# mLSTM readout: the epsilon and the negated mean of each tile's normalisation move from VectorE to GpSimd

## The chip, the cores and the metric

The kernel runs on one core of a Trainium2 chip. The metric is device time in microseconds (us) of one launch. Before the change the median of three runs is 2130.13 us (2129.56, 2130.13 and 2136.0). Engines are called as in the profile: PE (TensorE, with PEld for its weight loads), DVE (VectorE), ACT (ScalarE), POOL (GpSimd) and SP (SyncE, which issues the DMAs).

## What is computed

The kernel is one transformer block in float32: a gated feed-forward layer, a token mixer and a second feed-forward layer, over 1024 latent rows of 1024 values and 256 context rows. The mixer joins a bidirectional mLSTM with 4 heads of 128 and a banded attention with 8 heads, and multiplies the joined rows by an output matrix. The change touches only the readout of the mLSTM: each row of each head is normalised over its 128 values, and multiplied by a gain and an output gate.

```python
def _mlstm_readout(h, o_pre, g):
    mu = h.mean(-1, keepdims=True)
    var = jnp.square(h - mu).mean(-1, keepdims=True)
    hn = ((h - mu) * lax.rsqrt(var + LN_EPS)).reshape(B, T, M_WIDTH)
    return (hn * g * jax.nn.sigmoid(o_pre.astype(F32))).astype(o_pre.dtype)
...
y_l = jnp.concatenate([m_l, a_l], -1) @ w_out
```

## The kernel before

Every engine has one hand-written program, and the engines meet through semaphores. Rows are handled in tiles of 128, eight of them latent; `y_m` holds the mLSTM's output, 8 tiles of 4 heads by 128.

The mLSTM runs 16 latent steps (`for i in range(LAST)`), forward and backward in turn, so that tiles are finished in pairs from step 8 on. In a step, POOL scales the queries (`scaled`, L2836) and multiplies the scores by the decays (`probabilities`, L2844). PE multiplies queries by the state, updates the state and multiplies scores by values (all in the helper at L3078). ACT decays the state (L2907). DVE adds the update to the state (`carry`, L2997) and divides the sums by their denominators into `y_m` (`divide`, L3008 to L3018). PE starts step `i` only when the division of step `i - 2` has been done (`h_read`, as the steps share two PSUM regions) and when the carried state of two updates before is there.

The readout of a tile `q` (0 to 7, in the order `TILES_READ`) goes over three engines. Its parts are set into the engines' orders by hand:

- DVE, `stats_dve(q)`: four `bn_stats` (L2975) and four `bn_aggr` (L2982), one for each head, which leave mean and variance side by side in a small buffer; then a wait for the last of these, and two `scalar_tensor_tensor` of 128x4: minus the mean into `offset` (L2985) and the variance plus epsilon into `rate` (L2986). The last one raises `read_measured`. Tiles 0, 1 and 2 come in steps 10, 12 and 14, after `divide` and ahead of `carry`; tile 3 after the loop; 4 to 7 in `output_dve`, between the `out_row_low` instructions (L3249) that make the low parts of the rows for the output product. Two slots of the small buffer alternate, and from tile 2 on the aggregation waits for the normalisation of tile `q - 2`.
- POOL, `invert_pool(q)`: `rate` to the power of minus a half (L2870), a wait for that, and `offset` times `rate` (L2873); it raises `read_inverted` once for each.
- ACT, `readout_act(q)`: waits for both, and scales and shifts each head's rows in place (L2922, four instructions); it raises `read_normed`.
- POOL, `gated_pool(q)`: `y_m` times the gate rows `o_in` (L2879, 128x512); it raises `read_done`, which releases the load of the gate rows two tiles on (SP, `o_row_sp`) and PE's transposes.

POOL's order is: `scaled` and `probabilities` of steps 0 to 13, `invert_pool(0)`, those of step 14, `gated_pool(0)`, `invert_pool(1)`, those of step 15, `gated_pool(1)`, and then `invert_pool` and `gated_pool` of each tile from 2 to 7. ACT's order has `readout_act(0)` between the state's decays of steps 12 and 13, and `readout_act(1)` after that of step 13; from tile 4 on the readouts stand among the `row_high` instructions (L3207) and the two copies of the gate row (L3212).

On PE the output product (L3326 to L3328) follows the steps. Its first three parts use the attention's rows. Then come the transposes of `y_m` (`turn_rows`, L3312): those of units 4 and 5 wait for the gating of tile 3, and those of units 12 to 15, in the middle of the fifth output tile, for the gating of tile 7. After the output product come a normalisation and the second feed-forward layer.

Of the kernel before, what the change touches and what calls it, by code (L numbers as in the profile page):

```python
# [7 lines left out]
P = 128  # L8
# [3 lines left out]
ALU = mybir.AluOpType  # L12
# [13 lines left out]
LN_EPS = 1e-5  # L26
# [5 lines left out]
M_HEADS, M_DH, M_WIDTH = 4, 128, 512  # L32
# [18 lines left out]
def hybrid_block(nc, x, c, ctx, c_ctx, w_ada, b_ada, ln_g, ln_b, ffn_w13, ffn_w2, w_in, b_gates,  # L51
                 conv_w, conv_b, mh_norm_g, attn_sink, w_out, rope_cs, out):
    with ExitStack() as keep:
# [3 lines left out]
        def sem(name):  # L57
            return keep.enter_context(nc.semaphore(name))
# [25 lines left out]
        ones, minus_half = consts[:, 0:1], consts[:, 1:2]  # L84
# [2433 lines left out]
        def core_step(dve, instruction):  # L2518
            cstep[0] += 1
            instruction.then_inc(cores_step, 1)  # L2520
            dve.wait_ge(cores_step, cstep[0])
# [201 lines left out]
        read_measured = sem("read_measured")  # L2723
        read_inverted = sem("read_inverted")
# [104 lines left out]
        def mlstm_pool(pool):  # L2829
# [33 lines left out]
            for q in range(2, TL):  # L2863
                invert_pool(pool, q)
                gated_pool(pool, q)

        def invert_pool(pool, q):
            _, rate, offset = read_slots(q)
            pool.wait_ge(read_measured, q + 1)
            nc.gpsimd.tensor_tensor(rate, rate, minus_half[:, 0:1].to_broadcast([P, M_HEADS]), ALU.pow)\  # L2870
                .then_inc(read_inverted, 1)
            pool.wait_ge(read_inverted, 2 * q + 1)
            nc.gpsimd.tensor_tensor(offset, offset, rate, ALU.mult).then_inc(read_inverted, 1)  # L2873

        def gated_pool(pool, q):
# [34 lines left out]
        def read_slots(i):  # L2910

            at = 32 + 16 * (i % 2)
            return small[:, at:at + 8], small[:, at + 8:at + 12], small[:, at + 12:at + 16]

        def readout_act(act, q):

            t = TILES_READ[q]
            _, rate, offset = read_slots(q)
            act.wait_ge(read_inverted, 2 * q + 2)
            for h in range(M_HEADS):  # L2920
                rows = y_m[:, t, h * M_DH:(h + 1) * M_DH]
                last = nc.scalar.activation(rows, rows, ACT.Identity, bias=offset[:, h:h + 1], scale=rate[:, h:h + 1])  # L2922
            last.then_inc(read_normed, 1)
# [43 lines left out]
        def stats_dve(dve, q):  # L2967

            t = TILES_READ[q]
            dve.wait_ge(h_read, 1 + max(i for i in range(LAST) if STEPS[LAT0 + i][1] == t))  # L2970
            st = small[:, 8:32]
            mv, rate, offset = read_slots(q)
            by_head = mv.rearrange("p (h c) -> p h c", c=2)
            for h in range(M_HEADS):
                nc.vector.bn_stats(st[:, 6 * h:6 * h + 6], y_m[:, t, h * M_DH:(h + 1) * M_DH])\  # L2975
                    .then_inc(cores_step, 1)
                cstep[0] += 1
            dve.wait_ge(cores_step, cstep[0])
            if q >= 2:
                dve.wait_ge(read_normed, q - 1)  # L2980
            for h in range(M_HEADS):
                last = nc.vector.bn_aggr(mv[:, 2 * h:2 * h + 2], st[:, 6 * h:6 * h + 6])  # L2982
            core_step(dve, last)
            unit = ones.to_broadcast([P, M_HEADS])
            nc.vector.scalar_tensor_tensor(offset, by_head[:, :, 0], -1.0, unit, op0=ALU.mult, op1=ALU.mult)  # L2985
            nc.vector.scalar_tensor_tensor(rate, by_head[:, :, 1], LN_EPS, unit, op0=ALU.add, op1=ALU.mult)\  # L2986
                .then_inc(read_measured, 1)

        def cores_dve(dve):
            def carry(n):  # L2990
# [260 lines left out]

        def output_dve(dve):
            stats_dve(dve, 4)
            stats_dve(dve, 5)
            out_row_low(dve, 4)
# [552 lines left out]
```

## Time and profile before

| what | value |
| --- | --- |
| median of 3 runs | 2130.13 us |
| the profiled execution: span from its first to its last instruction | 2127.8 us |
| median less this span (what lies around the span) | 2.3 us |
| PE busy | 2091.4 us (98%) |
| DVE busy | 1527.0 us (72%) |
| ACT busy | 905.6 us (43%) |
| POOL busy | 192.8 us (9%) |
| mean granted clock of PE | 0.996 of full speed |
| steps 10 to 15 and the readout | about 1357 to 1406 us of the span |

Times in the profile count from the start of the span. A row of the timeline is one instruction, or several equal ones in a row (xN), with its start, its length, its engine, line, operation and operands; in brackets stands how long the engine had been idle before it and what released it. The profiled execution is known by its span alone; its own time is taken as the span and the 2.3 us that lie around it, which is the median.

### The profile page before, as it was taken

How to read it: one execution, taken by the hardware profiler on the slowest of the kernel's cores; microseconds unless marked ns; L12 is line 12 of the kernel's file. 1: busy time of each engine (PE TensorE's matmuls, PEld its weight loads, DVE VectorE, ACT ScalarE, POOL GpSimd, SP SyncE). 2: the span in 40 equal slices, each digit the busy share in tenths (PEclk: the TensorE clock that was granted, in tenths of full speed). 3: DMA queues.
4: the chain of work that ended last, by engine and by line, in shares of the span. 5: the costliest groups of instructions: out<-in, count | busy, mean ns of one | idle time of the engine just before them, and what ended most of it. 6: DMA issues, size and time to landing. Idle time of an engine off the chain costs nothing.

```text
span 2127.8 us, 31643 instructions
## 1 busy us (share of the span) xinstructions
PE 2091.4 (98%) x11508; PEld 1768.0 (83%) x11510; DVE 1527.0 (72%) x2520; ACT 905.6 (43%) x1631; POOL 192.8 (9%) x212
## 2 busy tenths in 40 slices
PE   8999999999999999999999999999999999999998
PEld 4888888888888888899878878877888888888886
DVE  5778888777648878675665465866867777767787
ACT  4622222222237446542565555734532323336445
POOL 0000000000000001090111002821000000000001
PEclk9999999999999999999999999999999999999999
DMA  8144444555459664733231002732244434349773
GB/s 298 33 142 147 149 134 129 160 167 159 129 186 348 193 215 148 209 101 117 74 108 41 21 21 66 182 109 99 75 134 140 136 104 153 123 139 341 257 234 112
DMA packets 261841, 310.38 MB, mean 146 GB/s; under 512 B 19350, under 2 KB 164686, under 8 KB 261710
## 3 DMA queue, kind: packets, MB, share of 16 engines
q1 hardware_dynamic: 261422, 308.52, 45.4%
q8 instruction: 80, 1.31, 0.2%
q14 instruction: 51, 0.42, 0.1%
q10 hardware_dynamic: 288, 0.13, 0.0%
HBM read 242.13 MB, written 66.45 MB: 145 GB/s over the span
## 4 chain that ended last, share of the span: by engine, by line
PE 86%; DVE 4%; DMA 3%; ACT 2%; issue 1%; POOL 1%; SPq 1%; DVEq 0%; POOLq 0%; ACTq 0%
PE psum L1327 11%; PE psum L1328 11%; PE psum L1329 11%; PE psum L1527 6%; PE psum L1529 6%; PE psum L1528 6%; PE psum L2056 3%; PE psum L2058 3%; PE psum L2057 3%; PE psum L1347 2%; PE psum L1346 2%; PE psum L1345 2%; PE psum L3078 2%; PE psum L875 2%; PE psum L876 2%; PE psum L877 2%
## 5 line engine op out<-in xcount | busy, mean ns | idle before, releaser
L1327 PE MATMUL psum<-x_mix_h,x_op_h 128*128 128x512 f32 x640 | 251.2, 393 | 1.3 <-DVE v_sum L1135 1.2
L1328 PE MATMUL psum<-x_mix_l,x_op_h 128*128 128x512 f32 x640 | 249.8, 390 | 0.0
L1329 PE MATMUL psum<-x_mix_h,x_op_l 128*128 128x512 f32 x640 | 249.5, 390 | 0.0
L1527 PE MATMUL psum<-s_high 128*128 128x512 f32 x616 | 240.0, 390 | 0.3 <-DVE s_low L1514 0.3
L1528 PE MATMUL psum<-s_low,s_high 128*128 128x512 f32 x616 | 239.9, 389 | 0.0
L1529 PE MATMUL psum<-s_high,s_low 128*128 128x512 f32 x616 | 239.9, 389 | 0.0
L1514 DVE TENSOR_TENSOR s_low<-s_raw,s_high 128x1024 fp32r<-128x1024 f32 x154 | 186.9, 1217 | 50.5 <-ACT s_high L1475 50.5
L1475 ACT ACTIVATE s_high<-s_raw 128x1024 fp32r<-128x1024 f32 x154 | 161.3, 1057 | 124.1 <-PE psum L1529 56.3
L1019 ACT ACTIVATE x_op_h<-raw 128x512 fp32r<-128x512 f32 x140 | 86.1, 627 | 203.6 <-PE psum L1329 121.1
L1019 ACT ACTIVATE x_op_h<-w_sum 128x512 fp32r<-128x512 f32 x160 | 97.1, 625 | 162.9 <-DVE w_sum L997 107.1
L1327 PEld LDWEIGHTS psum<-x_mix_h,x_op_h 128*128 128x128 f32 x640 | 120.4, 188 | 25.4 <-issue 1.8
L1329 PEld LDWEIGHTS psum<-x_mix_h,x_op_l 128*128 128x128 f32 x640 | 120.2, 188 | 25.3
L1328 PEld LDWEIGHTS psum<-x_mix_l,x_op_h 128*128 128x128 f32 x640 | 120.4, 188 | 23.2
L1527 PEld LDWEIGHTS psum<-s_high 128*128 128x128 f32 x616 | 115.7, 188 | 24.5 <-DVE s_low L1514 0.8
L1529 PEld LDWEIGHTS psum<-s_high,s_low 128*128 128x128 f32 x616 | 115.7, 188 | 24.2
L1528 PEld LDWEIGHTS psum<-s_low,s_high 128*128 128x128 f32 x616 | 115.7, 188 | 23.9
L1025 DVE TENSOR_TENSOR x_op_l<-raw,x_op_h 128x512 fp32r<-128x512 f32 x140 | 92.8, 686 | 39.2 <-ACT x_op_h L1019 37.0
L2056 PE MATMUL psum<-p_wh,xh_lat 128*128 128x256 f32 x384 | 111.7, 291 | 0.0
L2057 PE MATMUL psum<-p_wl,xh_lat 128*128 128x256 f32 x384 | 108.8, 283 | 0.0
L2058 PE MATMUL psum<-p_wh,xl_lat 128*128 128x256 f32 x384 | 108.8, 283 | 0.0
L1025 DVE TENSOR_TENSOR x_op_l<-w_sum,x_op_h 128x512 fp32r<-128x512 f32 x160 | 107.5, 683 | 0.0
L773 DVE SCALAR_TENSOR_TENSOR ada_sums<-ada_slice,more,ada_sums 128x512 f32<-128x512 f32 x140 | 99.6, 746 | 3.7 <-DVE ada_sums L773 0.5
(408 smaller groups left out, 5069.6 us busy)
## 6 DMA issues: line engine op xcount, KB each, us to landing
raw<-in_ffn_w SPq DMA_DIRECT2D x88, 512.0 KB, 5.4
f_terms<-g_half SPq DMA_DIRECT2D x154, 256.0 KB, 2.3
s_raw<-f_terms SPq DMA_DIRECT2D x154, 256.0 KB, 3.2
s_raw<-in_ffn_w SPq DMA_DIRECT2D x154, 256.0 KB, 4.0
ada_slice<-in_w_ada SPq DMA_DIRECT2D x112, 256.0 KB, 3.1
c_raw<-in_ffn_w SPq DMA_DIRECT2D x22, 512.0 KB, 3.5
p_raw<-in_w_in SPq DMA_DIRECT2D x22, 512.0 KB, 4.0
early<-in_w_ada SPq DMA_DIRECT2D x16, 512.0 KB, 6.6
```

What stands on the lines that cost most here:

```text
L1019: nc.scalar.activation(op_tiles(F, op)[0][:], OP_SOURCE[op], ACT.Copy).then_inc(F.hi, 1)
L1025: nc.vector.tensor_tensor(low[:], OP_SOURCE[op], high[:].bitcast(F32), ALU.subtract).then_inc(F.lo, 1)
L1327: nc.tensor.matmul(o, wh[:, k], high(k), start=i < 4 and k == 0, stop=False, skip_group_check=i > 3)
L1328: nc.tensor.matmul(o, wh[:, k], low(k), start=False, stop=False, skip_group_check=i > 3)
L1329: last = nc.tensor.matmul(o, wl[:, k], high(k), start=False, stop=k == KH - 1, skip_group_check=i > 3)
L1514: nc.vector.tensor_tensor(S.low[s % RING][:], S.raw[s % RAWS][:], S.high[s % RING][:].bitcast(F32), ALU.subtract)\
L1527: nc.tensor.matmul(o, h[:, 0, rows], h[:, 1], start=i == 0 and q in (0, 1, 6), stop=False, skip_group_check=True)
L1528: nc.tensor.matmul(o, h[:, 0, rows], l[:, 1], start=False, stop=False, skip_group_check=True)
L1529: return nc.tensor.matmul(o, l[:, 0, rows], h[:, 1], start=False, stop=i == PAIRS - 1, skip_group_check=True)
L2056: nc.tensor.matmul(o[:, 0:w], high, high_w[:, k, :], start=k == 0, stop=False)
L2057: nc.tensor.matmul(o[:, 0:w], high, low_w[:, k, :], start=False, stop=False)
L2058: last = nc.tensor.matmul(o[:, 0:w], low, high_w[:, k, :], start=False, stop=k == KD - 1)
```

## The change

VectorE's part of a tile ends with the four aggregations; the last of them raises `read_measured`. The wait for them and the two small instructions L2985 and L2986 are gone. POOL does their work at the head of `invert_pool`: it adds epsilon to the variances (read with a step of two) into `rate`, and multiplies the means by -1 into `offset`; each raises `read_inverted`, so that this semaphore counts four for each tile in place of two. The power waits for the first of them, the product for both and the power. VectorE waits, ahead of a tile's `bn_stats`, until its own aggregations of the tile before have landed, since these read the buffer that `bn_stats` overwrites.

```diff
         def invert_pool(pool, q):
-            _, rate, offset = read_slots(q)
+            mv, rate, offset = read_slots(q)
+            by_head = mv.rearrange("p (h c) -> p h c", c=2)
             pool.wait_ge(read_measured, q + 1)
+            nc.gpsimd.tensor_scalar_add(rate, by_head[:, :, 1], LN_EPS).then_inc(read_inverted, 1)
+            nc.gpsimd.tensor_scalar_mul(offset, by_head[:, :, 0], -1.0).then_inc(read_inverted, 1)
+            pool.wait_ge(read_inverted, 4 * q + 1)
             nc.gpsimd.tensor_tensor(rate, rate, minus_half[:, 0:1].to_broadcast([P, M_HEADS]), ALU.pow)\
                 .then_inc(read_inverted, 1)
-            pool.wait_ge(read_inverted, 2 * q + 1)
+            pool.wait_ge(read_inverted, 4 * q + 3)
             nc.gpsimd.tensor_tensor(offset, offset, rate, ALU.mult).then_inc(read_inverted, 1)
...
-            act.wait_ge(read_inverted, 2 * q + 2)
+            act.wait_ge(read_inverted, 4 * q + 4)
...
-            mv, rate, offset = read_slots(q)
-            by_head = mv.rearrange("p (h c) -> p h c", c=2)
+            mv, _, _ = read_slots(q)
+            if q:
+                dve.wait_ge(read_measured, q)
             for h in range(M_HEADS):
                 nc.vector.bn_stats(st[:, 6 * h:6 * h + 6], y_m[:, t, h * M_DH:(h + 1) * M_DH])\
                     .then_inc(cores_step, 1)
...
-            core_step(dve, last)
-            unit = ones.to_broadcast([P, M_HEADS])
-            nc.vector.scalar_tensor_tensor(offset, by_head[:, :, 0], -1.0, unit, op0=ALU.mult, op1=ALU.mult)
-            nc.vector.scalar_tensor_tensor(rate, by_head[:, :, 1], LN_EPS, unit, op0=ALU.add, op1=ALU.mult)\
-                .then_inc(read_measured, 1)
+            last.then_inc(read_measured, 1)
```

## Rows read from the trace of the kernel before

**Rows 1.** The page, part 1: busy time, share of the span and instructions.

```profile
PE 2091.4 (98%) x11508; PEld 1768.0 (83%) x11510; DVE 1527.0 (72%) x2520; ACT 905.6 (43%) x1631; POOL 192.8 (9%) x212
```

**Rows 2.** Stretches: length, then busy time (instructions) by engine, clock, DMA.

```profile
1357.00:1406.00 49.00, 44.00 (x263) 38.63 (x261) 38.72 (x147) 29.43 (x74) 32.19 (x34) 0.97 0.28 88
...
1480.00:2127.80 647.80, 638.31 (x2839) 528.60 (x2837) 481.44 (x655) 258.69 (x387) 10.50 (x11) 1.00 0.49 161
```

**Rows 3.** PE's waits, 1340 to 1480 us: total us, times, longest.

```profile
PE psum L3078 <- issue: 4.7, 4, 3.8
PE psum L3312 <- POOL y_m L2879: 1.2, 2, 0.6
```

**Rows 4.** Timeline of DVE around the first tile's statistics.

```profile
1359.51 0.38 DVE L2982 BATCH_NORM_AGGREGATE small<-small 128x2 f32<-128x6 f32 x4
1359.92 3.55 DVE L2985 SCALAR_TENSOR_TENSOR small<-small,consts 128x4 f32<-128x4 f32 x1
...
1363.47 0.68 DVE L2997 TENSOR_TENSOR state<-psum,state 128x516 f32<-128x516 f32 x1
```

**Rows 5.** Instructions on the small buffer: ns min/median/max, first and last start.

```profile
L2985 DVE SCALAR_TENSOR_TENSOR small<-small,consts x8: 161/744/3546, 1359.9 to 1396.2; 128x4 f32<-128x4 f32 x8
L2986 DVE SCALAR_TENSOR_TENSOR small<-small,consts x8: 148/152/156, 1363.4 to 1397.0; 128x4 f32<-128x4 f32 x8
L2870 POOL TENSOR_TENSOR small<-small,consts x8: 1007/1023/1454, 1363.6 to 1401.5; 128x4 f32<-128x4 f32 x8
```

**Rows 6.** Timeline of POOL over the readout.

```profile
1359.72 1.28 POOL L2844 TENSOR_TENSOR d_rows<-scores,d_rows 128x512 f32<-128x512 f32 x1
...
1362.18 1.27 POOL L2844 TENSOR_TENSOR d_rows<-scores,d_rows 128x512 f32<-128x512 f32 x1
1363.62 1.03 POOL L2870 TENSOR_TENSOR small<-small,consts 128x4 f32<-128x4 f32 x1 [0.17 <-DVE small L2986]
...
1366.11 1.26 POOL L2844 TENSOR_TENSOR d_rows<-scores,d_rows 128x512 f32<-128x512 f32 x1
1369.96 1.27 POOL L2879 TENSOR_TENSOR y_m<-y_m,o_in 128x512 f32<-128x512 f32 x1 [2.59 <-ACT y_m L2922]
...
1376.64 1.39 POOL L2870 TENSOR_TENSOR small<-small,consts 128x4 f32<-128x4 f32 x1 [0.46 <-DVE small L2986]
...
1381.53 1.39 POOL L2870 TENSOR_TENSOR small<-small,consts 128x4 f32<-128x4 f32 x1 [0.17 <-DVE small L2986]
...
1384.97 1.28 POOL L2879 TENSOR_TENSOR y_m<-y_m,o_in 128x512 f32<-128x512 f32 x1 [1.77 <-ACT y_m L2922]
...
1391.50 1.29 POOL L2879 TENSOR_TENSOR y_m<-y_m,o_in 128x512 f32<-128x512 f32 x1 [3.79 <-ACT y_m L2922]
...
1404.97 1.29 POOL L2879 TENSOR_TENSOR y_m<-y_m,o_in 128x512 f32<-128x512 f32 x1 [1.77 <-ACT y_m L2922]
```

**Rows 7.** Timeline of ACT: the first and the fifth tile's normalisation.

```profile
1368.25 1.64 ACT L2922 ACTIVATE y_m<-y_m,small 128x128 f32<-128x128 f32 x4
...
1389.78 1.64 ACT L2922 ACTIVATE y_m<-y_m,small 128x128 f32<-128x128 f32 x4
```

**Rows 8.** Timeline of PE.

```profile
1365.89 1.13 PE L3078 MATMUL psum<-state,q_rows 128*128 128x129 f32 x8 [3.81 <-issue]
...
1377.31 0.47 PE L3326 MATMUL psum<-wo_h,xh_lat 128*128 128x512 f32 x1
...
1386.39 1.07 PE L3312 MATMUL psum<-ident,y_m 128*128 128x128 f32 x8 [0.64 <-POOL y_m L2879]
...
1406.40 1.50 PE L3312 MATMUL psum<-ident,y_m 128*128 128x128 f32 x12 [0.59 <-POOL y_m L2879]
```

**Rows 9.** Stretch after PE's stall: columns as in rows 2.

```profile
1366.00:1371.00 5.00, 5.00 (x31) 5.00 (x32) 4.62 (x23) 2.82 (x8) 2.41 (x3) 0.66 0.01 3
```

**Rows 10.** POOL's lines by form: count, busy us, mean ns, idle before.

```profile
L2873 POOL TENSOR_TENSOR small<-small 128x4 f32<-128x4 f32 x8 | 1.7, 216 | 0.6
...
L3599 POOL MEMSET consts<- 128x1 f32 x1 | 0.1, 98 | 0.0
```

## The prediction, made before the changed kernel was run

> **What bounds the kernel now.** I read the page first: PE is busy for 98% of the span and DVE for 72% [rows 1]. So work taken from DVE is worth something only where PE waits. The table by stretches shows where it can be. After 1480 us PE is busy for 638.31 of 647.80 us, and in the readout's stretch for 44.00 of 49.00 us [rows 2]; the 5.0 us left there, and a lower clock, are all that the change can win. PE's waits name what it waits for: 4.7 us in the mLSTM's steps, 3.8 us of it at once, and 1.2 us for GpSimd's gating [rows 3]. None of the rows of that view for 1340 to 1480 us names a transfer.
>
> The timelines then tell why. DVE ends the first tile's aggregation at 1359.89 us and starts L2985, an instruction of 128x4 that takes 3.55 us [rows 4], where the same takes 0.16 us at its shortest [rows 5]. It ends when POOL's row of 128x512 products ends, at 1362.18 + 1.27 = 1363.45 us [rows 6]. Behind it on DVE stand the state's addition (1363.47 us, rows 4), then a division, and PE starts its next step at 1365.89 us after 3.81 us of idleness [rows 8]. In the 5 us after that the granted clock is 0.66 on average [rows 9], between its two levels of 1.2 and 2.4 GHz: 5 x 0.34 = 1.7 us of work at full speed lost.
>
> So one instruction costs PE about 3.4 us and the clock 1.7 us. But a second chain runs beside it and decides what comes out: POOL inverts, ACT normalises, POOL gates, tile after tile, and PE waits for it twice, 0.64 us at 1386.39 us and 0.59 us at 1406.40 us [rows 8]. The change takes from the first and adds to the second.
>
> **What is removed.** Eight pairs on DVE of about 0.16 + 0.15 us [rows 5]. Seven pairs lie beside other work of DVE, ACT and POOL; the first holds the 3.4 us. What was behind it (addition, division, PE's step 12) starts about 3.45 us earlier, PE at 1362.4 us, and with an idle time of a few tenths the clock should stay up. The new wait ahead of `bn_stats` is for DVE's own aggregations of a tile before, mostly long done; only tiles 4 and 5 follow each other directly, and there it stands for the wait that was removed between aggregation and L2985 (0.03 us, rows 4). I cost it at nothing; what is queued behind it is only DVE's row work, which ACT or PE outlast.
>
> The Trainium skill ("SBUF — State Buffer", Who interferes with whom) says that a VectorE instruction with two SBUF inputs and a GpSimd instruction that reads SBUF exclude each other, and that the second blocks until the first finishes. Here L2985 was let in only after three such products in a row, not after the first at 1361.00 us [rows 4, 6]. If the stall were the 1.0 us that the rule gives, the sum below would come to +0.2 us.
>
> **What is added.** Two instructions of 128x4 with one input and a constant, eight times, at the head of POOL's inversion. The trace of before has none of this kind. The nearest row is the 128x4 product L2873, 0.216 us on average with its dispatch overlapping its neighbour's [rows 10]; I take 0.15 us of POOL's time for each, so 0.30 us a tile. The lower end is the fill of one column, 0.098 us [rows 10], say 0.05 us of POOL's time. The upper end is the power, 1.02 us [rows 5]; I take the product, because both are plain arithmetic. The power's wait for the addition is covered by the second instruction, about as long as the rest of the first. Queued behind both on POOL are the products of steps 14 and 15 (for PE), and everything of the following tiles.
>
> **The sum, along POOL's order [rows 6].**
> 1. Tile 0. POOL is busy with step 13 until 1363.45 us in either kernel, so of the 3.4 us it gains nothing here: with 0.30 us of new work the power starts at 1363.75 us, 0.13 us later. Step 14's products end at 1366.11 + 1.26 + 0.13 = 1367.50 us. The gating waited 2.59 us more, until 1369.96 us, as ACT normalised only from 1368.25 us [rows 7], behind PE's late step. Now ACT can start at about 1365.2 us and end 1.64 us later, before POOL is free. The gating starts at 1367.50 us: **-2.46 us**.
> 2. Tile 1: +0.30 us, so -2.16 us for step 15's products and the gating.
> 3. Tile 2: POOL's wait of 0.46 us for DVE falls away, as DVE runs earlier by more, and 0.30 us comes: -2.32 us. The power's 1.39 us holds 0.37 us of waiting that I leave in.
> 4. Tile 3: 0.17 us of waiting away, 0.30 us added: -2.19 us. Its gating starts at 1384.97 - 2.19 = 1382.8 us, and PE's transposes, 1386.39 us before, at 1384.2 us. The output products ahead of them began at 1377.31 us and took some 8.4 us [rows 8]; they must begin by 1375.8 us, and step 15 lets them at about 1374 to 1375 us.
> 5. Tile 4: its gating waited 3.79 us where the others wait 1.77 us [rows 6], since ACT was kept by PE's transposes and the gate row. Those 2.0 us of slack cover the 0.30 us: -2.19 us stays. If the cover were gone, it would cost 0.30 us.
> 6. Tiles 5 to 7: from gating 4 at 1391.50 us to gating 7 at 1404.97 us the chain is closed, 13.47 us for three tiles. Each lengthens by 0.30 us: +0.90 us. The last gating starts 1.3 us earlier, and PE's last transposes at 1405.1 us in place of 1406.40 us.
>
> After that PE is nearly full [rows 2] and passes the gain on; SP's loads of gate rows and of the last weights follow the gatings and shift with them by 1 to 2 us, and PE waited for none [rows 3]. **Sum: -1.3 us.** The profiled execution spans 2127.8 us, which becomes 2126.5 us; the 2.3 us up to the median of 2130.13 us stay, so **2128.8 us**. A measurement of this kernel tells about 0.3% (6.4 us) from no change; -1.3 us (0.06%) is no change by it.
>
> **Rivals.**
> - *POOL's new instructions are dear (slower).* Its instructions have a floor that depends on the operation: the power takes 1.02 us for the same 128x4 [rows 5]. Of the 16 new ones 14 lie on the closed chain (all but tile 4's). At 1.02 us each it costs 14 x 0.87 = 12.2 us more than I take: -1.3 + 12.2 = +10.9 us, 2141.0 us. It becomes slower by over 0.3% from 0.15 + 7.7 / 14 = 0.70 us each. For it: no row shows this form. Against it: the product of the same size, with one operand more, takes 0.216 us. Chance 0.06. The Trainium skill ("GPSIMD Engine Reference", Engine selection) sends elementwise work to VectorE as about twice slower on GpSimd with two inputs and about equal with one; twice L2985's shortest would be 0.32 us, and by that, an estimate, the sum would be about +1 us. That no run here shows yet.
> - *The stall moves instead of going (about no gain).* With POOL busy without a break from 1360 to about 1375 us, the next DVE instruction with two operands that POOL's reads exclude, the first low part of the rows (L3249), arrives earlier and may be held as L2985 was, and in turn hold the powers, as the 0.37 us at 1376.64 and 1381.53 us suggests [rows 6]. Three such holds of 0.4 us and a late start of the output products of 1 to 2 us give -1.3 + 1.2 to +2: between 2130.0 and 2132.1 us. For it: those two powers. Against it: PE has over 1 us of room ahead of the transposes. Chance 0.16.
> - *The chain is looser than I read (more gain).* Then the whole stall and clock loss come out: -3.4 - 1.7 = -5.1 us, 2125.0 us. For it: both are in PE's own rows. Against it: POOL's order alone, with step 13 ending at 1363.45 us, bars it. Chance 0.07.
> - My forecast, with prices near the product's: 0.71.
>
> **How the numbers follow.** With the lower price the sum loses 14 x 0.10 = 1.4 us, and if the three long powers shrink to 1.02 us another 1.2 us: 2126.2 us. Above, the second rival ends at 2132.1 us. The range of 2126.2 to 2132.1 us holds the forecast and that rival, 0.87 less what executions scatter (one of three lay 5.9 us above the median). Faster by over 0.3% needs more than all that the third rival gives: 0.02. Slower by over 0.3% is the first rival's upper part and scatter: 0.06. The rest, 0.92, is no change.
>
> **What the profile should show.** L2985 and L2986 gone from DVE, and its state addition at about 1360 us right after the aggregation. PE's wait of 3.8 us gone, the clock at 1.00 from 1366 to 1371 us. On POOL two new lines of about 0.2 us, x8 each, and the wait of 2.59 us gone. PE's waits for the gating at L3312 longer, 2 to 3 us in place of 1.2 us: the same chain, now alone. The last gating between 1403 and 1405 us. I would be wrong if the new lines take over 0.4 us, if DVE shows another 128x4 or 128x512 instruction of 2 us and more in this stretch, or if the last gating comes after 1406 us.

## The result, and the profile after

The changed kernel is slower: 2134.31 us median against 2129.56 us (21 runs each; the 2130.13 us that the prediction started from was the median of three), a ratio of 1.0021 with a 95% interval of 1.0015 to 1.0028. That is 4.5 us by the ratio, against a forecast of -1.3 us, and the median lies outside the range of 2126.2 to 2132.1 us.

The profiled execution of the changed kernel took 2130.49 us, the shortest of its 21, with a span of 2128.3 us, and hardly differs from that of before (2127.8 us). Read by their spans the two traces would hide the loss, because the stretch ahead of the changed stage, the same code in every kernel here, takes a different time in each execution. So both are read from one point just ahead of the stage, the start of the second row of score products on POOL (**the entry** below), to the first product of the second feed-forward layer (**the layer**). In the fourteen traces of this case the entry lies anywhere between 1324.93 and 1332.44 us, while what comes behind that product takes 648.84 to 649.32 us in all of them. First before, timelines of POOL and of PE (the gatings 1, 2, 5 and 6, which [rows 6] leaves out, are POOL's products L2879):

```profile
1329.65 2.28 POOL L2844 TENSOR_TENSOR d_rows<-scores,d_rows 128x512 f32<-128x512 f32 x1
...
1374.90 1.28 POOL L2879 TENSOR_TENSOR y_m<-y_m,o_in 128x512 f32<-128x512 f32 x1
...
1380.07 1.29 POOL L2879 TENSOR_TENSOR y_m<-y_m,o_in 128x512 f32<-128x512 f32 x1 [1.76 <-ACT y_m L2922]
...
1395.80 1.30 POOL L2879 TENSOR_TENSOR y_m<-y_m,o_in 128x512 f32<-128x512 f32 x1 [1.76 <-ACT y_m L2922]
...
1400.22 1.29 POOL L2879 TENSOR_TENSOR y_m<-y_m,o_in 128x512 f32<-128x512 f32 x1 [1.76 <-ACT y_m L2922]
...
1478.52 0.50 PE L875 MATMUL psum<-xh_lat,f_h 128*128 128x512 f32 x1 [0.37 <-ACT x_quarter L360]
```

Then after, the same two timelines, with POOL's readout between (the new instructions are L2871 and L2872, the power L2874, the product of offset and rate L2877, the gating L2883):

```profile
1326.14 2.29 POOL L2844 TENSOR_TENSOR d_rows<-scores,d_rows 128x512 f32<-128x512 f32 x1
...
1364.30 1.27 POOL L2883 TENSOR_TENSOR y_m<-y_m,o_in 128x512 f32<-128x512 f32 x1
1365.66 0.24 POOL L2871 TENSOR_SCALAR small<-small 128x4 f32<-128x4 f32 x1
1365.97 0.23 POOL L2872 TENSOR_SCALAR small<-small 128x4 f32<-128x4 f32 x1
1366.16 1.05 POOL L2874 TENSOR_TENSOR small<-small,consts 128x4 f32<-128x4 f32 x1
...
1369.89 1.73 POOL L2883 TENSOR_TENSOR y_m<-y_m,o_in 128x512 f32<-128x512 f32 x1
...
1372.02 0.80 POOL L2872 TENSOR_SCALAR small<-small 128x4 f32<-128x4 f32 x1
...
1373.90 0.67 POOL L2877 TENSOR_TENSOR small<-small 128x4 f32<-128x4 f32 x1
1376.33 1.29 POOL L2883 TENSOR_TENSOR y_m<-y_m,o_in 128x512 f32<-128x512 f32 x1 [1.76 <-ACT y_m L2926]
...
1381.30 1.26 POOL L2883 TENSOR_TENSOR y_m<-y_m,o_in 128x512 f32<-128x512 f32 x1 [1.76 <-ACT y_m L2926]
...
1387.80 1.28 POOL L2883 TENSOR_TENSOR y_m<-y_m,o_in 128x512 f32<-128x512 f32 x1 [3.34 <-ACT y_m L2926]
...
1392.75 1.29 POOL L2883 TENSOR_TENSOR y_m<-y_m,o_in 128x512 f32<-128x512 f32 x1 [1.77 <-ACT y_m L2926]
1394.13 0.56 POOL L2871 TENSOR_SCALAR small<-small 128x4 f32<-128x4 f32 x1
1394.76 0.52 POOL L2872 TENSOR_SCALAR small<-small 128x4 f32<-128x4 f32 x1
...
1398.33 1.29 POOL L2883 TENSOR_TENSOR y_m<-y_m,o_in 128x512 f32<-128x512 f32 x1 [1.77 <-ACT y_m L2926]
...
1403.90 1.27 POOL L2883 TENSOR_TENSOR y_m<-y_m,o_in 128x512 f32<-128x512 f32 x1 [1.76 <-ACT y_m L2926]
```

```profile
1358.71 1.13 PE L3079 MATMUL psum<-state,q_rows 128*128 128x129 f32 x8
...
1368.85 1.13 PE L3079 MATMUL psum<-state,q_rows 128*128 128x129 f32 x8 [2.46 <-POOL q_rows L2836]
...
1382.70 1.06 PE L3313 MATMUL psum<-ident,y_m 128*128 128x128 f32 x8 [1.72 <-POOL y_m L2883]
...
1401.29 0.39 PE L3327 MATMUL psum<-wo_h,xh_lat 128*128 128x512 f32 x1
...
1405.31 2.79 PE L3313 MATMUL psum<-ident,y_m 128*128 128x128 f32 x12 [3.17 <-POOL y_m L2883]
...
1409.18 0.63 PE L3327 MATMUL psum<-wo_h,xh_lat 128*128 128x512 f32 x1
...
1479.46 0.50 PE L875 MATMUL psum<-xh_lat,f_h 128*128 128x512 f32 x1 [0.32 <-ACT x_quarter L360]
```

From the entry the layer begins after 1478.52 - 1329.65 = 148.87 us before and after 1479.46 - 1326.14 = 153.32 us in the changed kernel: **+4.45 us**. The measured loss has an interval of 3.2 to 6.0 us, so that one pair of traces meets its middle is chance. The table gives the starts of the gatings, tile by tile, from the entry in the same way (before: [rows 6] and the lines above; PE's transposes: [rows 8]).

| us from the entry | gating 0 | 1 | 2 | 3 | 4 | 5 | 6 | 7 | PE's last transposes | next layer |
| --- | --- | --- | --- | --- | --- | --- | --- | --- | --- | --- |
| before | 40.31 | 45.25 | 50.42 | 55.32 | 61.85 | 66.15 | 70.57 | 75.32 | 76.75 | 148.87 |
| after | 38.16 | 43.75 | 50.19 | 55.16 | 61.66 | 66.61 | 72.19 | 77.76 | 79.17 | 153.32 |
| difference | -2.15 | -1.50 | -0.23 | -0.16 | -0.19 | +0.46 | +1.62 | +2.44 | +2.42 | +4.45 |
| predicted | -2.46 | -2.16 | -2.32 | -2.19 | -2.19 | -1.89 | -1.59 | -1.29 | -1.3 | -1.3 |

The gain at the front came, and was almost gone by the third tile (gating 2). VectorE's part did what was said. Its timeline after shows the addition to the state at once behind the aggregation, 0.30 us after the aggregation's start where it was 3.96 us [rows 4]:

```profile
1356.01 0.38 DVE L2987 BATCH_NORM_AGGREGATE small<-small 128x2 f32<-128x6 f32 x4
1356.31 0.66 DVE L2998 TENSOR_TENSOR state<-psum,state 128x516 f32<-128x516 f32 x1
```

PE's waits after, 1340 to 1480 us (total, times, longest), answer to [rows 3]. The 4.7 us in the steps have become 2.8 us, nearly all of it a new wait for step 15's queries: PE, without its stall, gets there before POOL, which gates tile 0 and inverts tile 1 first, as before. The wait for the gatings went from 1.2 to 4.9 us:

```profile
PE psum L3313 <- POOL y_m L2883: 4.9, 2, 3.2
PE psum L3079 <- POOL q_rows L2836: 2.5, 1, 2.5
...
PE psum L3079 <- issue: 0.3, 1, 0.3
```

The last 2.0 us (4.45 less 2.42 us), between the transposes and the next layer, are PE's clock. After the wait of 3.17 us the output product runs near the lower of the clock's two levels: L3327 takes 0.63 us where it took 0.39 us ahead of the wait, and the stretch from 1406 us has a mean granted clock of 0.56 (columns as in [rows 2]). The stretch of the same times in run 4, told below, stands behind it:

```profile
1406.00:1412.00 6.00, 6.00 (x23) 5.19 (x22) 3.30 (x5) 2.29 (x4) 0.00 (x0) 0.56 0.71 188
```

```profile
1406.00:1412.00 6.00, 4.92 (x31) 3.85 (x30) 4.64 (x6) 3.53 (x6) 0.81 (x1) 1.00 0.37 106
```

### The profile page after: what moved, and what is told of

It is laid out like the page before. It is cut to its first block, busy times and chain, and to the rows that moved or that the text cites. A ratio compares the mean times of both kernels' runs of the same rounds, so it can differ in the third digit from the quotient of the medians.

```text
span 2128.3 us, 31652 instructions
## 1 busy us (share of the span) xinstructions
PE 2094.9 (98%) x11510; PEld 1771.0 (83%) x11510; DVE 1522.8 (72%) x2504; ACT 906.6 (43%) x1631; POOL 198.0 (9%) x228
## 4 chain that ended last, share of the span: by engine, by line
PE 90%; POOL 4%; DVE 2%; ACT 2%; DMA 1%; issue 1%; SPq 0%; DVEq 0%; POOLq 0%; ACTq 0%
PE psum L1328 12%; PE psum L1327 12%; PE psum L1329 12%; PE psum L1527 7%; PE psum L1528 7%; PE psum L1529 7%; PE psum L2056 3%; PE psum L2058 3%; PE psum L2057 3%; PE psum L1347 2%; PE psum L1346 2%; PE psum L1345 2%; PE psum L875 2%; PE psum L876 2%; PE psum L877 2%; PE psum L2483 1%
## 5 line engine op out<-in xcount | busy, mean ns | idle before, releaser
L1634 POOL TENSOR_TENSOR ln_stats<-ln_stats,consts 128x1 f32<-128x1 f32 x18 | 16.1, 897 | 953.4 <-DVE ln_stats L1629 953.4
```

## The experiments

The theory after the result has three parts. Each tile pays about 0.64 us for the two new instructions, and POOL and ACT take turns so closely that all of it but tile 4's reaches PE. Where VectorE's `out_row_low` instructions ("rows" below) come at the same time, the two engines hold each other up. And PE's longer wait lets its clock fall. The rivals are mutual holding alone, the clock alone, and chance. Every run was timed beside the kernel before; "layer" is the time from the entry to the next layer, read from each run's trace as above (before 148.87, after 153.32 us).

| run | median us | before beside it | ratio (95% interval) | layer us |
| --- | --- | --- | --- | --- |
| 1 two left out | 2125.01 | 2129.19 | 0.9982 (0.9973 to 0.9990) | 145.67 |
| 2 tile 0 only | 2125.84 | 2129.19 | 0.9984 (0.9974 to 0.9993) | 146.31 |
| 3 VectorE, one input | 2130.47 | 2129.19 | 1.0007 (0.9996 to 1.0017) | 148.90 |
| 4 filler | 2130.16 | 2129.19 | 1.0014 (0.9999 to 1.0029) | 151.36 |
| 5 early | 2125.65 | 2130.02 | 0.9978 (0.9966 to 0.9989) | 145.74 |
| 6 tile 0, early | 2127.13 | 2130.02 | 0.9983 (0.9971 to 0.9995) | 146.02 |
| 7 doubled | 2139.16 | 2130.02 | 1.0037 (1.0025 to 1.0048) | 158.13 |
| 8 rows later | 2129.69 (one run) | 2130.02 | none | 153.49 |
| 9 tile 0, early, gating 0 late | 2127.29 | 2129.78 | 0.9990 (0.9981 to 0.9999) | 147.58 |
| 10 early, gating 0 late | 2127.89 | 2129.78 | 0.9991 (0.9982 to 1.0000) | 148.81 |
| 11 one element | 2126.11 | 2129.78 | 0.9985 (0.9976 to 0.9995) | 145.77 |
| 12 one element, all tiles | 2122.73 | 2130.24 | 0.9959 (0.9945 to 0.9973) | 144.05 |

Chance is ruled out within the stage: up to gating 5 the gatings of after, run 4 and run 8, whose GpSimd programs are the same, agree within 0.02 us from the entry, and those of before and run 3 within 0.03 us up to gating 7. Where PE's clock falls is less sure (last section).

### 1. Without the two new instructions

```diff
-            nc.gpsimd.tensor_scalar_add(rate, by_head[:, :, 1], LN_EPS)...
-            nc.gpsimd.tensor_scalar_mul(offset, by_head[:, :, 0], -1.0)...
...
-            nc.gpsimd.tensor_tensor(rate, rate, minus_half..., ALU.pow)...
+            nc.gpsimd.tensor_tensor(rate, by_head[:, :, 1], minus_half..., ALU.pow)...
...
-            nc.gpsimd.tensor_tensor(offset, offset, rate, ALU.mult)...
+            nc.gpsimd.tensor_tensor(offset, by_head[:, :, 0], rate, ALU.mult)...
```

> The changed kernel without the two new GpSimd instructions: the power reads the variances and the product the means directly. It leaves out the epsilon and the minus sign. Theory (price on the chain): in the trace of after the two new instructions lengthen each tile's way from gating to power by about 0.6 us, on a chain that GpSimd and ScalarE close; without them the last gating comes about 3 us earlier than before, against the start of the steps, and the time is about 3 us below before (2126 to 2127.5 us, 7 us below after). Rival (contention): most of after's loss is that GpSimd and the two-operand row instructions of VectorE hold each other up; those stay, so at most half of that gain, 1 to 2 us below before. Rival (the changed order itself, whatever is added): as after, 4.5 us above before.

The last gating starts 72.10 us after the entry, 3.2 us sooner than before and 5.7 us sooner than after; the layer comes 3.20 us sooner than before. The removal from VectorE is worth that much, and the prediction had it right: with the new instructions at nothing, its sum is -1.3 - 7 x 0.30 = -3.4 us. The rival of holding alone fails, since holds are still there (gatings 1 and 2 take 1.74 and 1.60 us) and the gain is not halved. The two instructions, with what follows from them, cost 7.65 us of the layer's start (153.32 - 145.67).

### 2. Only the first tile on GpSimd

```diff
+        ON_POOL = 1
...
+            if q < ON_POOL:
+                nc.gpsimd.tensor_scalar_add(rate, by_head[:, :, 1], LN_EPS).then_inc(read_inverted, 1)
+                nc.gpsimd.tensor_scalar_mul(offset, by_head[:, :, 0], -1.0).then_inc(read_inverted, 1)
+                pool.wait_ge(read_inverted, done + 1)
...
+            if q < ON_POOL:
+                last.then_inc(read_measured, 1)
+                return
             core_step(dve, last)
             unit = ones.to_broadcast([P, M_HEADS])
```

These lines differ from the kernel before.

> GpSimd adds epsilon and negates for the first tile alone; the other seven tiles as before. Theory (price on the chain): the stall of 3.5 us of VectorE goes, and only one tile pays 0.6 us, so the first gating starts about 2 us earlier and most of it lasts: 1.5 to 2.5 us below before. Rival (the stall was hidden anyway, since GpSimd's own order decides): no difference from before. Rival (clock by chance): what a run gains or loses is where the clock falls; then a difference of under 1 us either way.

Gating 0 starts at 38.18 us and gating 7 at 72.74 us from the entry, 2.13 and 2.58 us sooner than before: the stall of VectorE was not hidden, and its gain lasts to the end where the other seven tiles do not pay.

### 3. VectorE with one input

```diff
-            nc.vector.scalar_tensor_tensor(offset, by_head[:, :, 0], -1.0, unit, ...)
-            nc.vector.scalar_tensor_tensor(rate, by_head[:, :, 1], LN_EPS, unit, ...)...
+            nc.vector.tensor_scalar_mul(offset, by_head[:, :, 0], -1.0)
+            nc.vector.tensor_scalar_add(rate, by_head[:, :, 1], LN_EPS)...
```

> The kernel before, with the two small VectorE instructions written with a constant in place of the second operand from the small buffer (tensor_scalar), all still on VectorE. Theory (the second SBUF operand makes VectorE wait for GpSimd's reads): the first of them takes about 0.15 us for every tile, the stall of 3.5 us and PE's wait of 3.8 us are gone, nothing is added on GpSimd: 2 to 3 us below before. Rival (any VectorE instruction on this buffer waits while GpSimd streams, or this form waits too): the stall of 3.5 us stays, no difference from before.

This is a change of the kernel before. Here the theory that the second operand makes the hold fell: the hold comes without it. The first of the two instructions took up to 3559 ns, as with two operands. This view is the one of [rows 5] (ns min/median/max):

```profile
L2984 DVE TENSOR_SCALAR small<-small x8: 170/752/3559, 1357.7 to 1394.0; 128x4 f32<-128x4 f32 x8
L2985 DVE TENSOR_SCALAR small<-small x8: 155/157/163, 1361.2 to 1394.8; 128x4 f32<-128x4 f32 x8
```

The Trainium skill agrees with the row ("SBUF — State Buffer", Who interferes with whom): `tensor_scalar` can enter a mode that uses both port pairs, and then it contends with GpSimd as well. Run 11 follows from that.

### 4. Filler on PE ahead of the last transposes

```diff
+            if u == 12:
+                for _ in range(24):
+                    nc.tensor.transpose(psum[:, YT_BANKS[u], 0:P], ident[:], ident[:])
             if k == 0:
                 pe.wait_ge(read_done, 4 if n else TL)
```

> The changed kernel with 24 further transposes of the identity on PE, into the bank that the next transposes overwrite, just ahead of its wait for the last gating: about 2.7 us of work in a wait of 3.2 us. Theory (the longer wait lets the clock fall): PE's clock stays at 1.00 after the last transposes, and the time is about 2 us below after, 2.5 us above before. Rival (the clock's fall after that wait costs nothing, as the chain behind has slack): as after, 4 to 5 us above before. Rival (the wait is shorter in most runs than in the profiled one): the filler delays PE, 5 us above before or more.

The gatings and the last transposes come as after, within 0.1 us (79.10 us from the entry), but the clock stays at 1.00 (the second of the two stretches above), the twelve transposes take 1.53 us in place of 2.79 us, and the layer comes 1.96 us sooner than after. So 2.0 us of the 4.45 us are the clock, after a wait that the chain made:

```profile
1406.86 1.53 PE L3316 MATMUL psum<-ident,y_m 128*128 128x128 f32 x12 [0.50 <-POOL y_m L2883]
```

That rests on the traces. The times cannot tell: the ratio is 3.0 us above before, with an interval from -0.2 to +6.2 us that holds both the theory's 2.5 us and after's 4.5 us.

### 5 and 6. Inversions in GpSimd's waits

```diff
-            gated_pool(pool, 1)
-            for q in range(2, TL):
-                invert_pool(pool, q)
+            for q in range(1, TL):
+                if q + 1 < TL:
+                    invert_pool(pool, q + 1)
                 gated_pool(pool, q)
```

Run 5 has this in the changed kernel, run 6 in the kernel of run 2.

> The changed kernel with GpSimd's order turned: the inversion of tile q + 1, with its two new instructions, stands ahead of the gating of tile q (from tile 2 on), in the 1.76 us in which GpSimd waits for ScalarE's normalisation. Theory (price on the chain): the new instructions cost because GpSimd and ScalarE take turns; in the wait they cost nothing, the last gating comes at or before PE's need, PE's wait of 3.2 us at the last transposes goes, and the time falls by 7 us against after, to 2 to 3.5 us below before. Rival (contention with VectorE's two-operand rows): the instructions are as long as after where rows and inversions meet, and at least half of the loss of 4.5 us stays. Rival (ScalarE or PE paces the tiles): the gatings keep a period of 4.4 us and more, 0 to 2 us below before.

> The first tile alone on GpSimd, as in the second run, and GpSimd's order turned as in the fifth. Theory (price on the chain): as the fifth run or up to 1 us better, 3 to 4.5 us below before, since nothing is left that the two instructions could cost from tile 1 on. Rival (VectorE's small instructions are held by GpSimd, which now has hardly a pause): they take 1 us and more each and push the rows' low parts back; no better than the second run, 2.5 us below before.

With the same instructions as after, run 5 starts the layer 7.58 us sooner than after and 3.13 us sooner than before. The turned order moves the whole inversion, the power and the product too, into GpSimd's waits. What the two instructions still cost there is read against run 6, which has this order and only the first tile's pair on GpSimd: 145.74 against 146.02 us, so the other seven pairs cost nothing. GpSimd's turns were the cost, not the instructions as such. In run 5 they still meet VectorE's rows: at tile 7 the two take 0.56 and 0.52 us in both kernels, so holding alone does not make the loss. PE's waits in run 5 no longer have one for the last transposes:

```profile
PE psum L3079 <- POOL q_rows L2836: 2.5, 1, 2.5
PE psum L3313 <- POOL y_m L2883: 1.9, 1, 1.9
```

Run 6 is not clearly better than run 5 or run 2 (its layer 0.28 us later and 0.29 us sooner), so the theory's further microsecond did not come. That is the rival's time, but not for its reason: the first of VectorE's two small instructions takes 0.16 to 1.07 us in run 6 and 0.16 to 1.09 us in run 2, no more than there. Gating 1 comes later than in run 2 (44.94 against 43.10 us from the entry), since an inversion now stands ahead of it, and PE waits 2.7 us for gating 3. From there on PE waits for no gating in either run, and paces both.

### 7. The two instructions twice

```diff
+            nc.gpsimd.tensor_scalar_add(rate, by_head[:, :, 1], LN_EPS)...
+            pool.wait_ge(read_inverted, 6 * q + 1)
+            nc.gpsimd.tensor_scalar_mul(offset, by_head[:, :, 0], -1.0)...
+            pool.wait_ge(read_inverted, 6 * q + 2)
             nc.gpsimd.tensor_scalar_add(rate, by_head[:, :, 1], LN_EPS)...
```

> The changed kernel with each of the two new GpSimd instructions issued twice (the second time with the same result). Theory (price on the chain): 0.6 us more a tile on seven of the eight tiles, the last gating 4.2 to 4.6 us later than after's against the start of the steps, and the time 4 to 5 us above after, 8 to 10 us above before. Rival (contention and the clock made after's loss, not the instructions): under 2 us above after.

The last gating starts at 83.35 us from the entry, 5.59 us later than after, and the layer 4.81 us later. The median is 4.85 us above after's, which was taken beside other runs of before, and the ratio is 7.9 us above before; the expected 8 to 10 us lie in its interval. The gatings of tiles 2 and 3 are 5.57 us apart, of after 4.97 us: 0.60 us for two more instructions, 0.30 us each. The 4.2 to 4.6 us that I expected for the gating were too few. From gating 3 to 4 it took 7.85 us in place of 6.50 us, as PE waited 3.1 us for gating 3 and its clock fell there, which the theory had left out; the eight transposes behind the wait took 1.94 us in place of 1.06 us:

```profile
1383.91 1.94 PE L3317 MATMUL psum<-ident,y_m 128*128 128x128 f32 x8 [3.11 <-POOL y_m L2887]
```

### 8. VectorE's rows out of the way

```diff
             readout_act(act, 5)
-            row_high(act, 8)
-            row_high(act, 9)
             readout_act(act, 6)
-            row_high(act, 10)
-            row_high(act, 11)
             readout_act(act, 7)
+            for u in range(8, 12):
+                row_high(act, u)
```

> The changed kernel with four high parts of rows on ScalarE (units 8 to 11), and so VectorE's two-operand low parts, moved behind the last normalisation. It delays PE's fifth output tile, so its time tells nothing; the gatings do. Theory with contention as the smaller part: from gating 5 to 6 and 6 to 7 the period falls from 5.58 and 5.57 us to that from 4 to 5, 4.95 us, as the new instructions take 0.23 us again in place of 0.56 and 0.52 us. Rival (no contention: the two are longer for their own reasons): the periods stay at 5.5 us.

POOL's timeline in this run, from gating 5 to gating 6, which stands above for after (1392.75 to 1398.33 us):

```profile
1391.80 1.29 POOL L2883 TENSOR_TENSOR y_m<-y_m,o_in 128x512 f32<-128x512 f32 x1 [1.76 <-ACT y_m L2926]
1393.17 0.23 POOL L2871 TENSOR_SCALAR small<-small 128x4 f32<-128x4 f32 x1
1393.48 0.23 POOL L2872 TENSOR_SCALAR small<-small 128x4 f32<-128x4 f32 x1
...
1396.76 1.29 POOL L2883 TENSOR_TENSOR y_m<-y_m,o_in 128x512 f32<-128x512 f32 x1 [1.77 <-ACT y_m L2926]
```

The period is 4.96 us for both tiles, and the new instructions take 0.23 us again. The rest of the 5.58 and 5.57 us, 0.62 and 0.61 us, is GpSimd held by VectorE's rows. As expected, the layer does not gain: PE now waits 4.5 us for the rows that were moved.

### 9 and 10. Gating 0 behind step 15

```diff
                 if i == LAST - 2:
-                    gated_pool(pool, 0)
                     invert_pool(pool, 1)
-            for q in range(1, TL):
-                if q + 1 < TL:
+            for q in range(TL):
+                if 0 < q < TL - 1:
                     invert_pool(pool, q + 1)
                 gated_pool(pool, q)
```

Run 9 has this in the kernel of run 6, run 10 in that of run 5.

> As the sixth run, with the gating of tile 0 moved behind step 15's products on GpSimd and all gatings one inversion back, so that PE gets the operands of its last step 1.3 us sooner. Theory (what is left of PE's waits is GpSimd's order): PE's wait for step 15 shrinks by about 1.3 us, but the wait for tile 3's gating, 2.7 us in the sixth run, takes it up, since the gatings come no sooner: within 1 us of the sixth run, 3 to 4 us below before. Rival (PE's start sets everything behind): 4 to 5.5 us below before.

> As the ninth run, with all tiles' epsilon and sign on GpSimd (the changed kernel with both moves of order). Theory: within 0.5 us of the fifth run, 3 to 5 us below before, as the two new instructions stand in GpSimd's waits. Rival (GpSimd is now so full that they cost again): 1 to 2 us slower than the ninth run.

PE got step 15's operands sooner, and waited for gating 3 all the same; gating 3 starts where it did (53.89 and 53.90 us from the entry, 53.88 us in run 6). Run 9's median is within 0.2 us of run 6's, as the theory said, but its 2.5 us below before are less than the expected 3 to 4 us. Run 10's is 1.9 us below before, where I expected 3 to 5 us. Its layer comes 3.1 us later than run 5's, and after PE's wait of 3.3 us for gating 3 its clock fell, which it did not in run 5 after 1.9 us. So earlier work on PE bought only a longer wait.

### 11 and 12. One element at a time on VectorE

```diff
-            nc.vector.scalar_tensor_tensor(offset, by_head[:, :, 0], -1.0, unit, ...)
-            nc.vector.scalar_tensor_tensor(rate, by_head[:, :, 1], LN_EPS, unit, ...)...
+            for h in range(M_HEADS):
+                nc.vector.tensor_scalar_mul(offset[:, h:h + 1], mv[:, 2 * h:2 * h + 1], -1.0)
+                last = nc.vector.tensor_scalar_add(rate[:, h:h + 1], mv[:, 2 * h + 1:2 * h + 2], LN_EPS)
```

This is a change of the kernel before; nothing moves to GpSimd. Run 11 has it for tile 0 only, run 12 for all tiles. Run 12 also inverts tiles 5, 6 and 7 one gating ahead, so it does not tell what each of its two changes is worth.

> The kernel before, where VectorE adds epsilon and negates the first tile's values one head at a time: eight instructions of 128x1 with a constant in place of two of 128x4. In the third run the one-input form of 128x4 was held for 3.56 us as the two-input one was. 
> The kernel before with the one-element instructions of the eleventh run for every tile, all on VectorE, and on GpSimd the inversion of tiles 5, 6 and 7 one gating ahead, in the waits for ScalarE (tiles 0 to 4 keep their order, so that the gating of tile 3 comes no later). Theory (the holds on VectorE and GpSimd's turns with ScalarE are the two things that PE waits for here): no instruction of VectorE's statistics takes over 0.2 us, PE does not wait at its last transposes, which come 0.6 to 0.8 us sooner than in the eleventh run against the start of the steps, and the time is 3.5 to 4.5 us below before. Rival (VectorE's eight instructions a tile cost what the holds did): no better than the eleventh run, 3 us below before.

In run 11 the eight instructions are let through while GpSimd streams, 0.49 us for all eight from the first start to the addition that follows:

```profile
1359.55 0.15 DVE L2986 TENSOR_SCALAR small<-small 128x1 f32<-128x1 f32 x1
...
1359.98 0.15 DVE L2987 TENSOR_SCALAR small<-small 128x1 f32<-128x1 f32 x1
1360.04 0.68 DVE L3003 TENSOR_TENSOR state<-psum,state 128x516 f32<-128x516 f32 x1
```

The layer comes 3.10 us sooner than before, nearly as much as in run 1 (3.20 us), which did none of this work at all; the median is 3.7 us lower, where I expected 2 to 2.5 us. Run 12 keeps that for every tile, and PE's wait for the last transposes is gone; in the view of PE's waits one row for gatings is left, the wait for gating 3:

```profile
L2988 DVE TENSOR_SCALAR small<-small x32: 141/144/155, 1362.7 to 1395.4; 128x1 f32<-128x1 f32 x32
L2989 DVE TENSOR_SCALAR small<-small x32: 140/144/146, 1362.8 to 1395.5; 128x1 f32<-128x1 f32 x32
```

```profile
PE psum L3315 <- POOL y_m L2882: 0.5, 1, 0.5
```

Its last transposes come 1.04 us sooner than run 11's from the entry and the layer 4.82 us sooner than before. It is the fastest of all, 0.9959 of before (0.9945 to 0.9973, from five runs). The ratio gives 8.7 us, more than the 3.5 to 4.5 us expected, and its trace explains 4.8 us of it. The rest is not settled. Of the five runs the profiled one took 2127.23 us and the other four 2122.28 to 2123.15 us. In the profiled one the entry comes at 1332.44 us, the latest of all traces, so it lost time ahead of the stage; what the other four did there no trace shows.

## Why the prediction was wrong, step by step

**What bounds the kernel** was read rightly: PE waits in two places, and of the two chains the one of POOL and ACT decides. The rival that this chain would become the bound had its place right and its price wrong. It was weighed at the power's 1.02 us an instruction, with a chance of 0.06. In between it named 0.70 us, from which the loss would pass 0.3%, and an estimate of 0.32 us, both with no chance of their own. That estimate met the measured price of 0.64 us a pair, but by luck: it doubles VectorE's time as for two inputs, and the new instructions have one.

**What is removed** was right. The hold of 3.4 us went, PE began its step 12 without a wait, and gating 0 came 2.15 us sooner, where step 1 of the sum had 2.46 us. Runs 1 and 11 show the gain by itself, 3.2 and 3.1 us at the next layer; run 2, which pays for one tile, has 2.6 us. One reading was off without harm: the eight pairs were taken at 0.16 + 0.15 us, the shortest, while [rows 5] has a median of 0.744 us for the first of a pair.

**What is added** was mis-sized, and this is the term that failed first: "I take 0.15 us of POOL's time for each, so 0.30 us a tile". It measured 0.64 us. The instruction itself takes 0.23 to 0.24 us, near the product's 0.20 us; what I missed is that it does not overlap its neighbours. In the rows of after, L2871 starts 0.09 us after the gating ends and L2872 0.07 us after L2871 ends, while the power behind L2872, like the 128x512 products, starts 0.04 to 0.05 us before the one ahead of it ends. From the end of the gating to the power's start it is 1366.16 - 1365.57 = 0.59 us after; before, the power came 0.05 us ahead of that end. No row of before had this form of instruction. But the row that the price came from already cost more than 0.15 us, as these lines of before, behind the power of [rows 6] at 1363.62 us, show:

```profile
1364.73 0.20 POOL L2873 TENSOR_TENSOR small<-small 128x4 f32<-128x4 f32 x1
1364.88 1.26 POOL L2836 TENSOR_TENSOR q_rows<-q_rows,qT 128x512 f32<-128x512 f32 x1
```

The power ends at 1364.65 us and the next instruction but one starts at 1364.88 us, 0.23 us later, where without the product it would have come 0.05 us before that end. So this product took 0.28 us of POOL's time: it overlaps its neighbour on one side only (it waits for the power ahead of it). In steps 2 and 6 the price shows plainly: from gating 0 to 1 and from 4 to 5, where VectorE's rows are not in the way, the tile lengthened by 0.65 us in place of 0.30 us. Run 7 gave the slope, 0.30 us for each further instruction.

**Step 3 (tile 2) and the second rival.** "0.30 us comes: -2.32 us" became -0.23 us, the largest single miss: +1.27 us for this tile in place of -0.16 us. Three of POOL's instructions there are long, gating 1 with 1.73 us, L2872 with 0.80 us and the product L2877 with 0.67 us, together 1.5 us more than elsewhere. VectorE's rows with two operands in SBUF run at just these times:

```profile
1369.73 0.77 DVE L3250 TENSOR_TENSOR xl_lat<-qaT,xh_lat 128x512 fp32r<-128x512 f32 x1 [1.35 <-ACT xh_lat L3208]
...
1372.05 0.68 DVE L3250 TENSOR_TENSOR xl_lat<-qaT,xh_lat 128x512 fp32r<-128x512 f32 x1
...
1373.85 1.27 DVE L3250 TENSOR_TENSOR xl_lat<-qaT,xh_lat 128x512 fp32r<-128x512 f32 x2
```

For this tile the cause is read from the times; no run moved these rows. Gating 1 is long in run 1 too (1.74 us), so that part comes without the new instructions. In tiles 6 and 7 holds came again, 0.62 and 0.61 us, and there run 8 shows the cause. The second rival had the two engines holding each other, with three holds of 0.4 us, and was given 0.16. I had added it as a rival to the cheap price; it came on top of a dear one.

**Step 5** was right: tile 4's slack covered its share (-0.16 us to -0.19 us). **Step 6** had +0.90 us for three tiles and got +2.63 us, by the two causes above.

**"After that PE is nearly full [rows 2] and passes the gain on"** left out the clock. I had priced it where the stall goes, and not where a new one comes. The forecast wait of 2 to 3 us for the gatings was in the text, but at no price; it became 1.72 and 3.17 us, and the second cost 2.0 us more (run 4).

The sum, then, starts from the forecast of -1.3 us. The price adds 7 x 0.34 = 2.4 us (all tiles but 4). The holds add 1.3 us, net of the long powers and the long product of before that went (0.37, 0.37, 0.12 and 0.43 us in tiles 2, 3, 6 and 7; the prediction had left the long powers in). The clock adds 2.0 us. Together that is +4.4 us. The price alone gives +1.1 us: it turned the sign, and the holds and the clock carried the time out of the range. The range was too narrow since its bounds moved one term at a time, though PE's longer wait, and with it the clock, follow from the dear instruction and the holds.

Two of the three signs of being wrong came: new lines of over 0.4 us (up to 0.80 us), and a last gating too late. The trace's 1403.90 us seems to meet the forecast of 1403 to 1405 us for that gating, but only because its entry came 3.51 us sooner; on the scale of before it is 1407.4 us.

## What to carry to other kernels

Where two engines take turns, every instruction moved onto one of them counts in full, once for each turn, however idle that engine is on average (here 9%). The same instructions in the wait between turns were free (run 5 against run 6), and turning the order was worth 7.6 us (run 5 against after). When a small instruction is held while another engine works, try another form before another engine: eight instructions of one element were not held where two of four were (run 11 against run 3). And a price carried over from another form of instruction should carry no overlap with its neighbours until a row shows it on both sides.

## What was not expected of the hardware

- GpSimd's `tensor_scalar` of 128x4 takes 0.23 to 0.24 us where it is not held, and starts 0.07 to 0.09 us after the instruction ahead of it ends, waiting for it (run 7) or not (after). The power, and the 128x512 products, start 0.04 to 0.05 us before that end; the 128x4 product, which waits for the power, takes 0.20 us and starts 0.08 us after it. The Trainium skill ("GPSIMD Engine Reference", Engine selection) has one-input work at roughly the line rate. At this size the runs show otherwise: 0.30 us of GpSimd's time for an instruction of four elements (run 7), against 0.08 us from one start to the next on VectorE for the same form where it is not held (run 3).
- VectorE's `tensor_scalar` of 128x4 from a strided buffer is held by GpSimd's 128x512 products for 3.56 us, over three of them in a row (run 3); eight of 128x1 between such products are not held (run 11).
- GpSimd's instructions are held too, when VectorE's rows with two operands in SBUF run: 0.56 and 0.52 us for 0.23 us (shown by run 8), and, read from the times alone, a gating of 1.73 us for 1.27 us.
- The clock does not follow from the length of the wait alone. After PE's wait of 2.7 us for gating 3 it fell in run 9 and not in run 6; the transposes behind it are the first and second line below. After the wait of 2.5 us for step 15 it fell in after and not in run 5 (the eight products behind it took 1.80 and 1.16 us). So one trace does not give the price of a wait of this length.

```profile
1384.91 1.94 PE L3327 MATMUL psum<-ident,y_m 128*128 128x128 f32 x8 [2.73 <-POOL y_m L2889]
```

```profile
1381.43 1.06 PE L3328 MATMUL psum<-ident,y_m 128*128 128x128 f32 x8 [2.71 <-POOL y_m L2890]
```
